# A bidirectional RWKV-7 scan on one NeuronCore: chunks of 128 tokens, direction by direction, against chunks of 64 tokens with both directions in one product

## The reference, cut to what matters

```python
def rwkv7_bidir_scan(r, w, k, v, kk, b):
    ...
    def step(s, inp):
        r_t, w_t, k_t, v_t, kk_t, b_t = inp
        sa = jnp.einsum('dbhvk,dbhk->dbhv', s, -kk_t)
        s = s * w_t[..., None, :] + sa[..., None] * b_t[..., None, :] + v_t[..., None] * k_t[..., None, :]
        return s, jnp.einsum('dbhvk,dbhk->dbhv', s, r_t)
    _, ys = lax.scan(step, s0, xs)
    ys = jnp.moveaxis(ys, 0, 2)
    return ys[0] + jnp.flip(ys[1], axis=1)

def rwkv7_mixer(p, ...):
    ...
    y = rwkv7_bidir_scan(rh, heads(w), heads(k_dir), vh, kk, b)
    mean = jnp.mean(y, axis=-1, keepdims=True)
    var = jnp.var(y, axis=-1, keepdims=True)
    y = (y - mean) * lax.rsqrt(var + RWKV_GN_EPS)
    y = y.reshape(y.shape[:-2] + (RWKV_WIDTH,)) * ln_w + ln_b
    bonus = jnp.sum(rh * heads(k_dir[0] + k_dir[1]) * r_k, axis=-1, keepdims=True) * vh
    return (y + bonus.reshape(y.shape)) * g
```

## Time and profile before

| | |
|---|---|
| median of 3 runs | 3662.59 us (3660.34 to 3702.36) |
| profiled execution, own time | 3687.77 us |
| its span | 3686.0 us |
| PE busy | 2898.9 us (79%) |
| DVE busy | 1643.6 us (45%) |
| ACT busy | 541.7 us (15%) |
| POOL busy | 369.0 us (10%) |
| mean granted clock of PE | 0.851 of full speed |

### The profile page before, as it was taken

How to read it: one execution, slowest core, us unless ns; L and a number is a source line. 1 busy time by engine, 2 the same in 40 slices (tenths; PEclk the granted TensorE clock), 3 DMA queues, 4 the chain that set the end, 5 groups by cost and what they waited for, 6 DMA issues and landing times. The chain is left out here.

```text
span 3686.0 us, 35596 instructions
## 1 busy us (share of the span) xinstructions
PE 2898.9 (79%) x14568; PEld 1854.9 (50%) x14568; DVE 1643.6 (45%) x2393; ACT 541.7 (15%) x742; POOL 369.0 (10%) x143
## 2 busy tenths in 40 slices
PE   5873679969967899996378365689898676798997
PEld 4663378859846545453266134534343454443343
DVE  6967465465553323234577555422121584312123
ACT  2121100010011111111422201200000213100001
POOL 3312010010010000000322223000000230000000
PEclk8986579868977899998689577789999887799998
DMA  5650000000012699993164101279999310699995
GB/s 169 215 181 0 9 1 1 1 1 1 1 46 117 288 411 415 415 410 155 46 217 149 41 0 46 120 316 427 428 428 427 104 54 23 263 427 428 428 427 238
DMA packets 136674, 725.36 MB, mean 197 GB/s; under 512 B 11878, under 2 KB 67174, under 8 KB 99367
## 3 DMA queue, kind: packets, MB, share of 16 engines
q1 hardware_dynamic: 112632, 700.98, 47.0%
q10 hardware_dynamic: 23920, 22.68, 1.9%
HBM read 721.53 MB, written 2.10 MB: 196 GB/s over the span
## 5 line engine op out<-in xcount | busy, mean ns | idle before, releaser
L1631 PE MATMUL ps<-s_c_ring,s_c_XG 128*64 128x512 f32 x2048 | 475.0, 620 | 80.2 <-DMA s_c_ring<-in_exp_w 62.6
L289 PE MATMUL ps<-s_h_part,s_w_hi 128*128 128x512 f32 x944 | 310.5, 412 | 63.9 <-PEq L413 63.0
L1631 PEld LDWEIGHTS ps<-s_c_ring,s_c_XG 128*64 128x64 f32 x2048 | 164.5, 142 | 384.8 <-issue 383.7
L273 POOL TENSOR_TENSOR s_w_lo<-s_w_raw,s_w_hi 128x2048 fp32r<-128x2048 f32 (+1 forms) x46 | 213.1, 4638 | 1279.6 <-ACT s_w_hi L266 1250.3
L1744 DVE TENSOR_TENSOR s_c_hid<-ps,s_c_sil 128x512 f32<-128x512 f32 x32 | 34.3, 1072 | 515.7 <-PE ps L1631 515.7
L289 PEld LDWEIGHTS ps<-s_h_part,s_w_hi 128*128 128x128 f32 x944 | 186.7, 200 | 105.8 <-issue 65.6
L1672 PE MATMUL ps<-s_c_ring,s_c_hidT 128*64 128x512 f32 x1024 | 223.3, 594 | 0.0
L1631 PE MATMUL ps<-s_m_ring,s_m_XG 128*64 128x512 f32 x1024 | 222.9, 593 | 0.0
L345 DVE SCALAR_TENSOR_TENSOR s_mod_acc<-s_mod_w,s_mod_silu,s_mod_acc 128x512 f32<-128x512 f32 x196 | 189.2, 965 | 47.4 <-DMA s_mod_w<-in_w_mod 38.5
L289 PE MATMUL ps<-s_h_part,s_w_lo 128*128 128x512 f32 x472 | 191.8, 406 | 0.0
L289 PE MATMUL ps<-s_src_part,s_w_hi 128*128 128x512 f32 x384 | 123.0, 402 | 42.7 <-DVE s_src_part L1262 29.2
(11 more groups left out here) (584 smaller groups left out, 4716.6 us busy)
## 6 DMA issues: line engine op xcount, KB each, us to landing
s_c_ring<-in_exp_w SPq DMA_DIRECT2D x192, 2048.0 KB, 17.3
s_m_ring<-in_moe_w_gate SPq DMA_DIRECT2D x32, 2048.0 KB, 12.0
s_m_ring<-in_moe_w_up SPq DMA_DIRECT2D x32, 2048.0 KB, 15.3
s_m_ring<-in_moe_w_down SPq DMA_DIRECT2D x32, 2048.0 KB, 12.4
s_mod_w<-in_w_mod SPq DMA_DIRECT2D x112, 512.0 KB, 5.0
s_w_raw<-in_w_in ACTq DMA_DIRECT2D x21, 1024.0 KB, 9.2
s_w_raw<-in_w_out SPq DMA_DIRECT2D x8, 1024.0 KB, 5.5
s_w_raw<-in_cf_w SPq DMA_DIRECT2D x16, 512.0 KB, 5.5
```

The source lines that it names most:

```text
L273: nc.gpsimd.tensor_tensor(self.lo[:, i % 2, :, at], self.raw[:, i % 2, :, at], self.hi[:, i % 2, :, at].bitcast(F32), ALU.subtract).then_i ...
L289: last = nc.tensor.matmul(bank, w[a][:, i % 2, k, c0:c0 + P], x[b][:, k, at], start=start, stop=stop)
L1631: last = nc.tensor.matmul(ps[x * SLOTS:(x + 1) * SLOTS, bank + fh, :], XG[:, k, c0:c0 + SLOTS], w[x][:, at:at + 512], start=(k == 0), stop ...
```

## The change

Chunks are 64 tokens (`RW_CHUNK`), 8 steps, 5 levels. Both directions go through the same step: the backward operands are written in flipped order, so that one set of masks serves both. A job is now 16 products: 8 blocks (2 directions x 4 feature groups) by 2 `rows`; each product has K=64 on one half of the partitions and writes 64 partitions of the same half, so the two that belong to a block stand in the upper left and the lower right quarter of PE's array, and both write the same PSUM bank (on different partitions). In U, X and Z only the half of the columns that is needed is formed (32 per block), and one evacuation takes all 16. That is 3808 products in 207 jobs. rhs, sa, b_tok, k_tok, v_tok and the first half of y are evacuated by ACT; POOL makes a diagonal matrix and the decayed state in each step (128x512 each).

`rwkv_prepare` replaces both calls of `rwkv_direction` and all transposes: it prepares both directions in one block, and the transposition to tokens is now a product in the scan (b_tok, k_tok with the diagonal matrix, v_tok). POOL does nothing in it. The product with `rw_r_k` moves there from `rwkv_output`. The mask tensor shrinks from 2304 to 1248 columns.

```diff
-LEVELS = 7
+RW_CHUNK, RW_LEVELS = 64, 6
...
+        def rwkv_prepare(proj, kk, w2, a2, kd_sum, bufs, reset):
...
+                        for d in range(2):
+                            rows = slice(64 * d, 64 * d + 64)
+                            for j in range(2 * CT):
+                                if d == 1:
+                                    pe.wait_ge(act_out.sem, a0 + j + 1)
...
+                            if d == 1:
+                                act.wait_ge(dve_out.sem, v0 + PER_DVE)
+                            for j in range(2 * CT):
...
+                                nc.scalar.activation(dst[:, c, :], ps[:, j, :], ACT.Sigmoid, bias=vcol(name, c)).then_inc(*act_out.up())
...
+                            for c in range(CT):
+                                ins = nc.scalar.activation(kd[:, c, :], a_[:, c, :], ACT.Identity, bias=keep[:, c:c + 1], scale=vcol("rw_k_a", c))
...
+                            nc.scalar.activation(flat(ex), flat(cc), ACT.Exp, scale=decay).then_inc(*act_out.up())
...
+                            nc.scalar.activation(flat(sg), flat(sg), ACT.Exp, scale=-decay).then_inc(*act_out.up())
...
+                            nc.scalar.activation(flat(cc), flat(cc), ACT.Exp, scale=-decay).then_inc(*act_out.up())
...
+                                ins = V.tensor_tensor_scan(x, reset, s, 0.0, ALU.mult, ALU.add)
+                            ins.then_inc(*dve_out.up())
+                            dve.wait_ge(dve_out.sem, vd + 2)
+                            V.tensor_tensor(flat(sg), flat(cc), flat(sg), ALU.subtract).then_inc(*dve_out.up())
+                            dve.wait_ge(act_out.sem, ad + 2 * CT + 1)
+                            vlink(V.tensor_tensor(flat(kd), flat(kd), flat(k_), ALU.mult))
+                            V.tensor_tensor(flat(a_), flat(a_), flat(kk), ALU.mult)
...
+                            vlink(V.tensor_tensor(k, kd[:, :, :], ex[:, :, :], ALU.mult))
+                            V.scalar_tensor_tensor(b, a_[:, :, :], -1.0, ex[:, :, :], ALU.mult, ALU.mult)
...
+                            V.tensor_tensor(q, kk[:, :, :], sg[:, :, :], ALU.mult)
...
+                            ins = V.tensor_tensor(r, r_[:, :, :], cc[:, :, :], ALU.mult)
+                            if d == 1:
+                                vlink(ins)
+                                ins = V.tensor_tensor(flat(kd_sum), flat(kd_sum), flat(kd2), ALU.add)
...
+            jobs = [("A", 0, 0, 0), ("N", 0, 0, 0)]
+            for j in range(N_STEP):
+                last = j > 0
+                for l in range(1, TOP + 1):
+                    one, two = [], []
+                    if l == 1:
+                        one, two = [("rhs", j - 1, 0, 0)] if last else [], [("RB", j, 0, 0)]
+                    elif l == 2:
+                        one, two = [("sa", j - 1, 0, 0)] if last else [], [("BT", j, 0, 0)]
+                    elif l == 3:
+                        one, two = [("S", j - 1, 0, 0)] if last else [], [("b_tok", j, 0, 0)]
+                    elif l == 4:
+                        one, two = [("RK", j, 0, 0)], [("A", j + 1, 0, 0), ("N", j + 1, 0, 0)] if j + 1 < N_STEP else []
+                    else:
+                        one, two = [("k_tok", j, 0, 0), ("v_tok", j, 0, 0)], [("y", j - 1, 0, 0)] if last else []
+                    jobs += [("U", j, 0, l)] + one
+                    jobs += [("X", j, 0, l)] if l < TOP else []
+                    jobs += [("Z", j, 0, l)]
+                    jobs += two
+            jobs += [(name, N_STEP - 1, 0, 0) for name in ("rhs", "sa", "y")]
...
+                            if name in ("A", "N", "RB", "BT", "RK"):
...
+                                for h, (w, c) in enumerate(blocks):
+                                    for r in rows:
+                                        last = mm(bank[r, h * C:(h + 1) * C], lhs[r, w, c, at], rhs_[r, w, c, at], start=True, stop=True)
...
+                            elif name == "U":
+                                after(*(("N", j, 0, 0) if l == 1 else ("X", j, d, l - 1)))
+                                for h in range(BLK):
+                                    for r in rows:
+                                        last = mm(bank[r, h * (C // 2):(h + 1) * (C // 2)], N[r, h, :], part(X[r, h:h + 1, :], l, 0)[:, 0], start=True, stop=True)
...
+                            nc.gpsimd.tensor_tensor(diag2[j % 2][:], bcast(same, BLK), t, ALU.mult).then_inc(pool_did.sem, 1)
...
+                                nc.gpsimd.tensor_tensor(S2[(j + 1) % 2][:], S2[j % 2][:], t, ALU.mult).then_inc(pool_did.sem, 1)
...
+                            elif name == "U":
+                                mask = level(l).rearrange("p (m b) -> p m b", b=2 ** l).unsqueeze(1).to_broadcast([P, BLK, C // 2 ** (l + 1), 2 ** l])
+                                ins = tt(part(U[l][:], l, 0), halves(i, l), mask, ALU.mult)
+                            elif name in ("X", "Z"):
+                                M = part(X[:], l, 0) if name == "X" else part(Z[:], l, 1)
+                                ins = tt(M, M, halves(i, l), ALU.add)
...
         def rwkv_output(proj, y, kd_sum, g2, ahead):
...
-                        for c in range(CT):
-                            nc.vector.scalar_tensor_tensor(kd_sum[:, c, :], r_[:, c, :], vcol("rw_r_k", c), kd_sum[:, c, :], ALU.mult, ALU.mult).then_inc(*dve_out.up())
```

More of the change, by code:

```diff
@@ new lines, in build @@
+                        old = again(proj[:, 0:8, :], 8) + again(kk[:, :, :], 4)
+                        for n in ("X", "Z", "N", "RB", "RK", "v_tok"):
+                            bufs[n] = [old.pop(), old.pop()]
+                        for n in ("S", "diag"):
+                            bufs[n] = [sbuf(scan, "rw_" + n, [P, 2 * CT, RW_CHUNK]) for _ in range(2)]
+                        bufs["U"] = {l: sbuf(scan, "rw_U", [P, 2 * CT, RW_CHUNK]) for l in range(1, RW_LEVELS)}
+                        for n in ("BT", "rhs", "sa", "b_tok", "k_tok"):
+                            bufs[n] = sbuf(scan, "rw_" + n, [P, 2 * CT, RW_CHUNK])
```

506 lines of the change are left out of this document (245 added, 261 removed).

## The result

The changed kernel takes 3361.75 us (median of 4 runs, 3347.47 to 3384.42) against 3667.36 us (4 runs, 3660.34 to 3702.36) in the same session: ratio 0.9141, 95% interval 0.9089 to 0.9193. The forecast was 3356 us. Its profiled execution took 3372.33 us, 315.4 less than the 3687.77 of before.

A forecast was written before the change was run, and what follows sets the result against it. PE was taken to bound the scans. From 3687.8 us, 268 (scan), 32 (preparation) and 6 (output stage) came off, giving 3382 profiled; the median lying 25 us lower, the forecast was 3356 us, range 3300 to 3530.

The forecast's parts named there:

- PE sets the pace: In the scans, PE was busy 256.5 us each; only its time per product or the number of products could shorten them.
- 58 ns for a product, 32 or 64 columns alike: Scan products at full clock: 58 ns whatever the column count, 107 at half clock; 3808 products make 221 us.
- the rival of the columns: Scan jobs U, X, Z: fewer moving columns do count, 29 ns a product, 52 us less, about 3300 us; chance 0.06.
- Two quarters at once, in one bank: Scan: two diagonal 64x64 products overlap although they write one PSUM bank, giving 58 ns for each product.
- the rival on it: Scan: quarters sharing a bank don't overlap; 3544 us at full clock, 3925 at half; chance 0.04 and 0.05.
- Clock: Scan starts at 1.2 GHz; with a rise in step 0 or 1, 250 to 300 products cost 107 ns: +14 us.
- The first rival: Clock stays at 1.2 GHz through the scan: 422 us there, 3524 in total; chance 0.15, throughout or mostly.
- Waits: Scan: PE waits for DVE in step 0, level 5, and the last rhs, sa and y; +14 us.
- GpSimd beside VectorE: Scan: two POOL passes a step slow DVE passes, mostly hidden; 0 to +45 us, taken as +6 us.
- The scan's sum: Scan: 221 + 14 + 14 + 6 = 255 us against 522.6 before, a saving of 268 us.
- Preparation: One block for both directions takes 62 us instead of 47.7 + 46.4, a saving of 32 us.
- Output stage: Removing the four L978 passes saves 6 us, not 10, because the square root covers the remainder.

The follow-up runs named there:

- full columns: Changed kernel with U, X and Z forming all 64 columns of each block instead of the 32 needed; 3349.39 us, ratio 0.9082 to the kernel before.
- One quarter alone: Changed kernel with every scan product on partitions 64-127 left out, so half the work is missing; 3554.11 us in one run.
- halves apart: Changed kernel with each scan job issuing its eight products on partitions 0-63 first, then the eight on 64-127; 3770.74 us in one run.

## Why the prediction was right, step by step

- **PE sets the pace.** PE is busy for 210 of 212 us behind step 0, and 7 to 26 us more of VectorE's work (three kernels) and twice GpSimd's lengthened the scan by half a microsecond at most, the clock taken out. Right.
- **58 ns for a product, 32 or 64 columns alike.** 58 ns measured in both kinds; full columns cost nothing; halving the columns bought nothing. Right, and with it the rival of the columns is out. Over the whole fast part it is 59.7 ns with all waits in it (213.3 us for 3570 products), 59.3 without the last two, so the stream is 226 us rather than 221. Of the 5 us, 2 are the wait for VectorE in level 5. (The 16 records of the earlier trace rows are two jobs, and the evacuation at 529.88 is that of the first; the price read from them stands.)
- **Two quarters at once, in one bank.** This was the step without a row, and the rival on it had 0.09. It holds, though nothing in the rows said so: 0.09 was a judgement and no measurement. One quarter alone at 217 ns and halves apart at 174 show what its failure would have cost: the rival's price, 214 ns, was right, and by the order of issue alone the change would indeed have been slower than before.
- **Clock.** Predicted to rise in the middle of step 0 or in step 1, +14 us. It rose for good 31 us into the scan, late in step 0, and held: 238 products at 110 instead of 59 ns are 12 us. Not foreseen was the first rise at 3.7 us, which was lost in the pause before the first U. That the size came out is luck in part: with the pause filled the same products had their full clock from 3 us on. The first rival (half clock throughout) did not come about with both quarters busy; with one it did.
- **Waits.** +14 us forecast, 6.4 measured (3.3 before the first U, three of 0.53 in step 0, two of 0.7 to 0.8 at the last rhs and sa). The five passes of A and N ahead of U in level 5, which I had left open, cost 0.3 us in each of seven steps; these 2 us lie between records that overlap and are counted in the stream here.
- **GpSimd beside VectorE.** +6 us forecast from passes of 1.6 us; they take 1.04 us, and twice as many cost nothing in the later steps. What it cost is 1.2 us in step 0, part of the 3.3 us of waiting above. Mis-sized, near the low end of the bounds.
- **The scan's sum** was 255 us (221 + 14 + 14 + 6) and came to 244.4 (226 + 12 + 6.4 + 0). The forecast took 522.6 us as the old scans' length and looked at their clock no further.
- **Preparation.** 62 us forecast, 58.3 measured. The first direction took 31.2 of 32 us; all of the error is in the second, 26.5 instead of 30. Its four cumulative sums took 4.6 us where up to 6.4 were allowed. The rest is the forecast's own sum: the terms that it names for that direction (6.4 + 16 + 3) make 25.4 and not 30, those of the first 28.7 and not 32, and it doesn't say what the rest stands for. The unnamed 3 us of the first direction were there; those of the second, all but 1, weren't. Reversed writes cost nothing (2.29 us a pass in both directions).

```profile
L747 DVE TENSOR_TENSOR_SCAN s_rw_cc<-s_masks,s_rw_sg 128x512 f32<-128x512 f32 x8 | 9.5, 1215 | 4.7 <-ACT s_rw_sg L710 4.7
```

- **Output stage.** -6 us forecast, -5.8 measured, with the square root as the cover that was named.
- **The sum** for the profiled execution was 3382 and its own time 3372.3. The median was 11 us below that where I had taken 25, and the two errors nearly cancel: 3361.75 against 3356. The hit is closer than the terms were, and that closeness is luck: the runs of either kernel spread over 37 to 42 us.

## What to carry to other kernels

Where PE sets the pace with small float32 products, ask what a product costs by its weight load and by how many of the array's quarters work at once: two diagonal 64x64 quarters halved the price, and halved output columns did nothing where both quarters were kept busy. Write the products of different quarters alternately, one and one: the same products in groups of eight cost three times as much, by lost overlap and by the clock that stays down. Then look at where PE pauses in the first microseconds at half clock; filling a 3 us pause with later jobs was worth 2.5 us in itself and 9 us by the clock, in the scan's own length; in whole times it didn't show. A busy share near 100% doesn't exclude a short wait in every step: follow one step through the timeline.

## What the runs showed of the hardware that was not expected

- **PE starts products out of the program's order across quarters, but not far.** With the halves apart, records of y (L896) start at 701.35 while three of Z (L870) ahead of them in the program are still to come, and about three products of a group find a partner (58, 59, 59, 67 ns for groups of one, two, three, four; 174 at half clock for eight). The Trainium skill, "TensorE: Matmul & The Clock Gate", section "The mechanism", says that only weight loads are pulled ahead and that products start in strict order; the starts in these traces are not in order.
- **PE busy nearly all the time, and the clock at its lower level.** With one quarter PE was busy for 407.7 of 414.1 us and the granted clock stayed at 0.50; with both quarters in turns of eight, 657.4 of 662.5 us, again 0.50; in turns of one it reached 1.00. With turns of four it did too, after 45 us. What in the work makes that difference these runs don't show.
- **When the clock rises for good isn't settled.** 31, 31, 31, 31, 24, 24, 16 and 14 us after the scan's start in kernels whose step 0 differs little, each time but one (16) after a first rise at 3 to 4 us that was lost in the pause before U. In the two that fill the pause that first rise held for 24 us, was lost for 3.4 us behind a pause of 1.9, and came back. Whether the same kernel rises at the same point each time wasn't tried, and what makes 14 out of 31 stays open.
- **GpSimd slows some VectorE passes and not others.** Passes of 128x512 that read and write no PSUM took 1.38 and 1.22 us beside it and 0.69 without; those that read PSUM took 0.69 beside it too.
- **The stages ahead vary.** The stages ahead of the preparation, untouched in all thirteen kernels, took 418 to 455 us in the profiles; a whole-kernel time can't show an edit of 10 us beside that.
